# A two-block transformer kernel in split fp32: drain waits, the order of a product's passes, and the places of constants, a recurrent step and latent means

## The chip, the cores and the metric

The kernel runs on one core of a Trainium2 chip. The metric is the device time of one execution, in microseconds; lower is better. A core has TensorE (PE in the profile, with its weight loads as PEld), VectorE (DVE), ScalarE (ACT), GpSimd (POOL) and SyncE (SP). Each works through its own list of instructions in order; they meet at semaphores. SP and ACT also issue DMA transfers, each on a queue of its own.

## What is computed

A sequence of 256 tokens with 1024 channels passes through two blocks, each with two layers. All matrices are fp32.

```python
def first_block(x, ...):                      # per layer
    h = _rmsnorm(x, norm1_g[layer])
    proj = h @ w_in[layer]                    # split into the heads' parts
    o_a = _hgrn2(...)                         # gated recurrence, chunks of 64
    o_b = _nsa(...); o_c = _fox(...)          # two kinds of attention
    x = x + concatenate([o_a, o_b, o_c]) @ w_o[layer]
    h2 = _rmsnorm(x, norm2_g[layer])
    x = x + square(relu(h2 @ w_up[layer])) @ w_down[layer]

def second_block(x, c, ctx, c_ctx, ...):      # per layer; hc is the context stream
    h = h + HALF * gt1 * swiglu(ada_norm(h, g_ffn1[l], sh1, sc1), w1, w3, w2)
    u = ada_norm(h, g_mix[l], sh2, sc2)
    z_conv, z_cq, z_ckv, z_kr, z_four = split_mixing(u @ w_in[l])
    # latent attention: rms_norm(z_cq) @ w_uq, rms_norm(z_ckv) @ w_ukv
    y = merge_branches(u, conv_module(z_conv, ...), attn @ w_o_mla[l],
                       fourier_mix(z_four, ...), w_bgate[l], b_bgate[l], w_out[l])
    h = h + gt2 * y
    h = h + HALF * gt3 * swiglu(ada_norm(h, g_ffn2[l], sh3, sc3), w1, w3, w2)
```

`swiglu` is `(silu(x @ w1) * (x @ w3)) @ w2`; `merge_branches` is `(g0*y_conv + g1*y_mla + g2*y_four) @ w_out` with sigmoid gates. In the second block's first layer the context stream goes through the same steps, so the tiles there are 512 wide (256 tokens of each stream); in its second layer most are 256 wide.

## The kernel before

**Weights.** The weights come as one stream of chunks, mostly 128 x 1024 fp32 (512 KB: eight tiles of 128 x 128), through a ring of four slots. SP issues each load (L2614) when PE has released the slot (`used`). `PLAN` gives each product its place in the stream: `in_t`, `up`, `down`, `ffn1`, `ffn1_out`, `conv_in`, `lat_in`, `mix_out` and so on. A product has `n` groups of 128 output channels, each with one to four chunks.

**Split products.** Where a product is split, a chunk is made into two parts: ACT copies it, rounded, into `w_hi` (`split_high`, L749), and DVE writes the rest, `w_lo`, over the ring slot (`split_low`, L773). The activations are split in the same way (`hn_hi`/`hn_lo`, `hid_hi`/`hid_lo`, `mrg_hi`/`mrg_lo`). `split_product` (L802) makes three matmuls for each of the eight tiles: low weights by high activations (L812), high by high (L815), high by low (L818). Before, all eight of L812 come first and then the pairs. Parts are made some groups ahead (`splits_ahead`, `early`, `shift`).

**Banks.** Groups alternate between two pairs of PSUM banks. `wait_banks` makes PE wait until the group two before has been drained; `wait_all_drained` waits for the last two groups of a product.

**Feed-forward of the second block.** `gated_pair` makes 22 groups of ffn1 or ffn2. ACT applies Silu to one bank, DVE multiplies by the other (L2160, which frees the banks), copies to `hid_hi` (L2163) and subtracts for `hid_lo` (L2166). Then comes the out-projection (`hidden_product`), whose first chunk reads rows 0 to 7.

**Merging.** The last branch, mrg_mla, ends for each of 8 groups with a gate (L2263), an addition (L2269, which frees the banks), the copy to `mrg_hi` (L2273) and the subtraction to `mrg_lo` (L2275). mix_out reads all eight rows in its first group, each behind a wait for its `mrg_lo`.

**in_t with the recurrence.** block1 makes 18 groups of in_t on PE while DVE and ACT run the recurrence in turns tied to group numbers: in group 3 DVE does the forget gate (`hg_start_dve`, L1306 to L1313, which needs ACT's two sigmoids of L1405/L1406), in group 5 the scan, and from group 6 on a step every two groups: two subtractions (`hg_grow_dve`, L1341/L1345), an exponential on ACT (L1414), two products (`hg_decay_dve`, L1361/L1362), sixteen small matmuls on PE (`hg_pe`, L1276), and the taking of the scores (`hg_take_dve`, L1374), for which PE's next step waits. In each group DVE first makes the low part that is due and then the step's work.

**Start.** x, the small constants and the parameters are loaded first. ACT issues the large constants (L1617) and the context (L1618) after the first norm. DVE needs the constants in group 3 of in_t, PE in group 7.

**Latent part.** After conv_in (three groups of two chunks) come ten groups of lat_in, while DVE runs 31 convolution taps (L2523, L2526). ACT copies each group into z (L2417) and squares some. PE then makes two means (L2309, L2312), ACT turns each into a reciprocal root (L2426, L2428), and PE and ACT run the Fourier steps: step u writes bank 4 + u % 2 (L2200, second stage L2208), ACT copies it (L2218), and step u waits for copy u - 2; the second stage waits for all copies of the first. There are 8 first-stage steps in layer 0 and 4 in layer 1. DVE applies the roots (`latent_normed`) at tap 22.

Of the kernel before, what the change touches and what calls it, by code (L numbers as in the profile page):

```python
# [30 lines left out]
T = 256  # L31
# [515 lines left out]
def kernel_program(nc, streams, consts, params, x_cm, ctx_cm, out_cm, blocks=(1, 2)):  # L547
    with ExitStack() as stack:
# [253 lines left out]
        def split_product(pe, lin, g, c, dst, wait_part, x_hi, x_lo, start=True, stop=True, order=None):  # L802

            wait_split(pe, lin, g, c)
            slot = slot_of(lin, g, c)
            order = order or range(lin.tiles[c])
            for k in order:
                if g.at == 0:  # L810
                    wait_part(0, k)
                pe.matmul(dst, w_lo[slot][:, k * P:(k + 1) * P], x_hi(k), start=(start and k == order[0]), stop=False)  # L812
            for k in order:
                high = w_hi[:, slot, k * P:(k + 1) * P]
                pe.matmul(dst, high, x_hi(k), start=False, stop=False)  # L815
                if g.at == 0:
                    wait_part(1, k)
                mm = pe.matmul(dst, high, x_lo(k), start=False, stop=(stop and k == order[-1]))  # L818
            mm.then_inc(used[slot], 1)
# [792 lines left out]
        def block1_act(act, l):  # L1612
            if l == 0:
                first_split(split_high, act, PLAN["in_t", 0])
            norm_act(act, 2 * l, PLAN["in_t", l], PLAN["down", l - 1] if l else None)
            if l == 0:
                act.dma_start(con12[:, 0:CONST_SETS[1][1]], consts[1]).then_inc(s.consts1, 16)  # L1617
                act.dma_start(res[:, :, T:2 * T], ctx_cm).then_inc(s.ctx_in, 16)  # L1618
                act.wait_ge(s.lb, 1)
                act.activation(lb, lb, ACT.Exp).then_inc(s.lb, 1)  # L1620
# [70 lines left out]
            norm_act(act, 2 * l + 1, PLAN["up", l], PLAN["wo", l])  # L1691
            if l == DEPTH - 1 and 2 in blocks:
                act.wait_ge(s.norm_value, KT * 2 * DEPTH)
                act.dma_start(con12[:, 0:CONST_SETS[2][1]], consts[2]).then_inc(s.consts2, 16)
                act.dma_start(par12[:, 0:PARAM_SETS[2][1]], params[2]).then_inc(s.consts2, 16)
                act.dma_start(crow, params[3]).then_inc(s.crow_in, 16)
# [111 lines left out]
        def block1_dve(dve, l):  # L1808
# [6 lines left out]
            for m in range(lin.n):  # L1815
                splits_ahead(split_low, dve, lin, Group(m, m, 0, period(1)))
                if m == SLOT_F and l == 0:
                    dve.wait_ge(s.consts1, 16)
                hg_dve(dve, l, m)
            for m in range(2):  # L1820
                hg_dve(dve, l, IN_SLOTS + m)
# [273 lines left out]
        def ffn_pe(pe, l, which):  # L2095
            n = 2 * DEPTH + 3 * l + which
            w = norm_width(n)
            lin = PLAN["ffn1" if which == 0 else "ffn2", l]
            norm_pe(pe, n)
            gated_pair(pe, lin, n, w)  # L2100
            wait_all_drained(pe, lin)
            lin = PLAN["ffn1_out" if which == 0 else "ffn2_out", l]
            for g in turns(pe, lin):
                wait_banks(pe, lin, g)
                hidden_product(pe, lin, g, FF2 * (2 * l + which // 2), w)
# [85 lines left out]

        def fourier_pe(pe, l):
            wait_all_drained(pe, PLAN["lat_in", l])
            for u, stage, a, tt, gp in fourier_steps(l):
# [17 lines left out]

        def fourier_act(act, l):
            for u, stage, a, tt, gp in fourier_steps(l):
# [77 lines left out]
        def block2_pe(pe, l):  # L2292
# [14 lines left out]
            pe.wait_ge(s.c_sq, l + 1)  # L2307
            for k in range(3):
                mm = pe.matmul(bank[6][:, 0:w], const(2, "ones_ct"), q2[:, 3 + k, 0:w], start=(k == 0), stop=(k == 2))  # L2309
            mm.then_inc(s.c_ms, 1)  # L2310
            for k in range(2):
                mm = pe.matmul(bank[7][:, :], const(2, "ones_kv"), q2[:, 6 + k, :], start=(k == 0), stop=(k == 1))  # L2312
            mm.then_inc(s.c_ms, 1)
# [76 lines left out]
            wait_all_drained(pe, PLAN["mrg_mla", l])  # L2390
            lin = PLAN["mix_out", l]
            for g in turns(pe, lin):
                wait_banks(pe, lin, g)
                split_product(pe, lin, g, 0, bank[2 * parity(lin, g)][:, 0:w],
                              lambda part, k: pe.wait_ge(s.mrg_lo, KT * l + k + 1),
                              lambda k: mrg_hi[:, k, 0:w], lambda k: mrg_lo[:, k, 0:w])
            ffn_pe(pe, l, 2)

        def block2_act(act, l):
# [24 lines left out]
            for i, (b, wi) in enumerate(((6, w), (7, 2 * T))):  # L2424
                act.wait_ge(s.c_ms, 2 * l + i + 1)
                act.activation(tmp3[:, i, 0:wi], bank[b][:, 0:wi], ACT.Ln, bias=eps_col)  # L2426
                act.drain()
                last = act.activation(tmp3[:, i, 0:wi], tmp3[:, i, 0:wi], ACT.Exp, scale=-0.5)  # L2428
            last.then_inc(s.c_rs, 1)
# [71 lines left out]
        def block2_dve(dve, l):  # L2501
# [6 lines left out]
            for g in turns(dve, lin, tail=2):  # L2508
                splits_ahead(split_low, dve, lin, g)
# [6 lines left out]
            if seqs(l) == 1:  # L2516
                first_split(split_low, dve, PLAN["lat_in", l])
# [211 lines left out]
```

## Time and profile before

| | us |
|---|---|
| median of 3 runs | 2947.27 (2946.25 to 2950.39) |
| profiled execution | 2950.16 |
| its span, first to last instruction | 2948.4 |
| mean granted TensorE clock | 0.987 |

| engine | busy us | share of the span |
|---|---|---|
| PE | 2840.2 | 96% |
| DVE | 1644.5 | 56% |
| ACT | 1124.3 | 38% |
| POOL | 48.1 | 2% |

The span is that of the profiled execution; its own time is 1.8 us longer. PE is busy nearly all the time, so the other engines' idle time costs nothing unless PE waits for them. A clock of 1.00 is TensorE's full clock (2.4 GHz), 0.50 is half of it (1.2 GHz).

### The profile page before, as it was taken

The numbers are of one execution on the slowest core, as the hardware profiler recorded it, in microseconds if no ns is written. First come the engines' busy times: TensorE is split into PE (matmuls) and PEld (weight loads), VectorE is DVE, ScalarE is ACT, GpSimd is POOL, SyncE is SP. The second block draws the span as 40 slices with busy tenths as digits, with TensorE's granted clock in tenths as the row PEclk, the third lists the DMA queues.
The fourth block names the chain that finished last, engine by engine and source line by source line (L and its number), as shares of the span: only waits on it lengthen the run. The fifth ranks groups of instructions, "written<-read, shape, count | busy, mean of one in ns | idle before, by whom it ended". The sixth has DMA issues, their size and how long they took to land.

```text
span 2948.4 us, 44779 instructions
## 1 busy us (share of the span) xinstructions
PE 2840.2 (96%) x16592; PEld 2370.8 (80%) x16592; DVE 1644.5 (56%) x2829; ACT 1124.3 (38%) x1715; POOL 48.1 (2%) x36
## 2 busy tenths in 40 slices
PE   7999999999999999999999999999999998999998
PEld 7759998659998888785666778888788887788998
DVE  6547656447666555677334476555533336745665
ACT  4345534345542222324544232222322223584443
POOL 0100001000000000030000000000000000000000
PEclk9999999999999999999999999999999999999999
DMA  5574554655544343321221233433322222234454
GB/s 186 182 247 144 184 182 130 221 210 196 185 157 145 140 150 128 121 91 40 76 68 54 96 112 139 149 133 132 105 94 98 91 96 98 89 112 144 164 183 152
DMA packets 118357, 400.08 MB, mean 136 GB/s; under 512 B 12896, under 2 KB 20960, under 8 KB 117856
## 3 DMA queue, kind: packets, MB, share of 16 engines
q1 hardware_dynamic: 115120, 391.43, 39.1%
q10 hardware_dynamic: 3120, 7.07, 0.7%
q8 instruction: 76, 1.25, 0.2%
q14 instruction: 41, 0.34, 0.0%
HBM read 397.40 MB, written 1.05 MB: 135 GB/s over the span
## 4 chain that ended last, share of the span: by engine, by line
PE 84%; DVE 6%; DMA 3%; ACT 3%; issue 2%; DVEq 1%; POOL 1%; SPq 0%; ACTq 0%; POOLq 0%
PE bank L812 23%; PE bank L815 22%; PE bank L818 22%; PE bank L2234 4%; DMA ring<-weights 3%; PE bank L1534 2%; DVE w_lo L773 1%; PE bank L1979 1%; PE bank L1959 1%; DVE hn_lo L1019 1%; DVE work L2048 1%; PE bank L899 1%; ACT w_hi L749 1%; PE bank L1463 1%; POOL w_lo L773 1%
## 5 line engine op out<-in xcount | busy, mean ns | idle before, releaser
L773 DVE TENSOR_TENSOR w_lo<-ring,w_hi 128x1024 fp32r<-128x1024 f32 (+1 forms) x538 | 650.0, 1209 | 720.8 <-ACT w_hi L749 718.5
L749 ACT ACTIVATE w_hi<-ring 128x1024 fp32r<-128x1024 f32 (+1 forms) x548 | 571.4, 1044 | 1172.5 <-DMA ring<-weights 1172.2
L815 PE MATMUL bank<-hn_hi,w_hi 128*128 128x256 f32 (+1 forms) x2816 | 885.1, 334 | 0.0
L818 PE MATMUL bank<-hn_lo,w_hi 128*128 128x256 f32 (+1 forms) x2816 | 884.6, 334 | 0.0
L815 PEld LDWEIGHTS bank<-hn_hi,w_hi 128*128 128x128 f32 x2816 | 536.9, 191 | 52.2
L818 PEld LDWEIGHTS bank<-hn_lo,w_hi 128*128 128x128 f32 x2816 | 536.8, 191 | 52.2
L812 PE MATMUL bank<-hn_hi,w_lo 128*128 128x256 f32 (+1 forms) x2816 | 559.0, 341 | 15.0 <-DVE w_lo L773 5.6
L812 PEld LDWEIGHTS bank<-hn_hi,w_lo 128*128 128x128 f32 x2816 | 445.5, 191 | 84.7 <-issue 19.8
L815 PE MATMUL bank<-hid_hi,w_hi 128*128 128x512 f32 (+1 forms) x704 | 248.7, 363 | 0.0
L818 PE MATMUL bank<-hid_lo_a,w_hi 128*128 128x512 f32 (+1 forms) x640 | 226.2, 363 | 0.0
L812 PE MATMUL bank<-hid_hi,w_lo 128*128 128x512 f32 (+1 forms) x704 | 156.8, 363 | 4.9 <-DVE work L2160 4.9
L815 PEld LDWEIGHTS bank<-hid_hi,w_hi 128*128 128x128 f32 x704 | 132.9, 189 | 20.6
L812 PEld LDWEIGHTS bank<-hid_hi,w_lo 128*128 128x128 f32 x704 | 121.7, 189 | 26.7 <-issue 5.1
L818 PEld LDWEIGHTS bank<-hid_lo_a,w_hi 128*128 128x128 f32 x640 | 120.8, 189 | 18.7
L815 PE MATMUL bank<-up_hi,w_hi 128*128 128x256 f32 x512 | 125.6, 283 | 0.0
L818 PE MATMUL bank<-up_lo,w_hi 128*128 128x256 f32 x512 | 125.6, 283 | 0.0
L2234 PE MATMUL bank<-hid,ring 128*128 128x512 f32 (+1 forms) x352 | 124.2, 494 | 1.3 <-ACT hid L2023 1.3
L2526 DVE SCALAR_TENSOR_TENSOR hid<-work,par,hid 128x512 f32<-128x512 f32 (+1 forms) x180 | 117.4, 707 | 5.0 <-issue 0.5
L815 PEld LDWEIGHTS bank<-up_hi,w_hi 128*128 128x128 f32 x512 | 98.3, 192 | 0.0
L818 PEld LDWEIGHTS bank<-up_lo,w_hi 128*128 128x128 f32 x512 | 98.3, 192 | 0.0
L2234 PEld LDWEIGHTS bank<-hid,ring 128*128 128x128 f32 x352 | 63.8, 189 | 42.7 <-issue 38.3
L1456 PE MATMUL bank<-hn_hi,w_lo 128*128 128x256 f32 (+1 forms) x160 | 63.5, 405 | 28.4 <-ACT hn_hi L994 16.9
(320 smaller groups left out, 3006.3 us busy)
## 6 DMA issues: line engine op xcount, KB each, us to landing
ring<-weights SPq DMA_DIRECT2D x692, 512.0 KB, 3.3
ring<-weights SPq DMA_DIRECT2D x32, 384.0 KB, 3.0
ring<-weights SPq DMA_DIRECT2D x32, 256.0 KB, 2.6
ring<-weights SPq DMA_DIRECT2D x28, 192.0 KB, 2.3
con<-consts ACTq DMA_DIRECT2D x1, 2063.0 KB, 7.4
con<-consts ACTq DMA_DIRECT2D x1, 1088.0 KB, 5.0
res<-ctx_cm ACTq DMA_DIRECT2D x1, 1024.0 KB, 14.1
con<-params ACTq DMA_DIRECT2D x1, 1024.0 KB, 7.1
```

The source lines that it names most:

```text
L749: act.activation(w_hi[:, slot, 0:w], ring[slot][:, 0:w], ACT.Copy).then_inc(s.w_hi, 1)
L773: eng.tensor_tensor(w_lo[slot][:, 0:w], ring[slot][:, 0:w], w_hi[:, slot, 0:w].bitcast(F32), ALU.subtract).then_inc(s.w_lo, 1)
L812: pe.matmul(dst, w_lo[slot][:, k * P:(k + 1) * P], x_hi(k), start=(start and k == order[0]), stop=False)
L815: pe.matmul(dst, high, x_hi(k), start=False, stop=False)
L818: mm = pe.matmul(dst, high, x_lo(k), start=False, stop=(stop and k == order[-1]))
L899: mm = pe.matmul(ada_bank(h)[rows, :], cs[:, k, COND_AT - 2 * q:COND_W - 2 * q], ring[slot][:, i * 4 * P:(i + 1) * 4 * P], start=(q == 0 a ...
L1019: last = dve.scalar_tensor_tensor(out=hn_lo[:, k, t], in0=sq[:, k, t], scalar=modulation(l)[:, SHIFT[which], k, c:c + 1], in1=hn_hi[:, k, ...
L1456: pe.matmul(dst[c], w_lo[slot[c]][:, k * P:(k + 1) * P], hn_hi[:, k, 0:w], start=(k == 0), stop=False)
L1463: mm = pe.matmul(dst[c], w_hi[:, slot[c], k * P:(k + 1) * P], hn_lo[:, k, 0:w], start=False, stop=(k == KT - 1))
L1534: mm = pe.matmul(bank[2 * parity(lin, g)][:, q], sq[:, k, q], ring[slot_of(lin, g, 0)][:, k * P:(k + 1) * P], start=(k == 0), stop=(k == K ...
L2234: mm = pe.matmul(bank[2 * parity(lin, g)][:, 0:w], ring[slot_of(lin, g, 0)][:, k * P:(k + 1) * P], src[:, k, 0:w], start=(k == 0), stop=(k ...
L2526: last = dve.scalar_tensor_tensor(out=dst, in0=src, scalar=taps[:, m, k:k + 1], in1=dst, op0=ALU.mult, op1=ALU.add)
```

## The change

- `ffn_pe` and `block2_pe` no longer call `wait_all_drained` between ffn1/ffn2 and the out-projection and between mrg_mla and mix_out.
- `split_product` can go row by row (`by_row`): for each tile its low pass and its two high passes. mix_out uses it.
- ACT issues the large constants behind its first high part, ahead of the first norm, and the context after the second norm of the first layer.
- In in_t, DVE does the recurrent step of a group ahead of the low part due in that group.
- The latent means move into the Fourier steps on PE, ahead of step 2; on ACT the roots move ahead of the copy of step 3.
- In the last layer, the first low part of lat_in moves into conv_in's last group, ahead of its gate.

```diff
-        def split_product(pe, lin, g, c, dst, wait_part, x_hi, x_lo, start=True, stop=True, order=None):
+        def split_product(pe, lin, g, c, dst, wait_part, x_hi, x_lo, start=True, stop=True, order=None, by_row=False):
...
-            for k in order:
+            def low_pass(k):
                 if g.at == 0:
                     wait_part(0, k)
                 pe.matmul(dst, w_lo[slot][:, k * P:(k + 1) * P], x_hi(k), start=(start and k == order[0]), stop=False)
-            for k in order:
+
+            def high_passes(k):
                 high = w_hi[:, slot, k * P:(k + 1) * P]
                 pe.matmul(dst, high, x_hi(k), start=False, stop=False)
                 if g.at == 0:
                     wait_part(1, k)
-                mm = pe.matmul(dst, high, x_lo(k), start=False, stop=(stop and k == order[-1]))
-            mm.then_inc(used[slot], 1)
+                return pe.matmul(dst, high, x_lo(k), start=False, stop=(stop and k == order[-1]))
+
+            if by_row and g.at == 0:
+                for k in order:
+                    low_pass(k)
+                    mm = high_passes(k)
+            else:
+                for k in order:
+                    low_pass(k)
+                for k in order:
+                    mm = high_passes(k)
+            mm.then_inc(used[slot_of(lin, g, c)], 1)
...
         def block1_act(act, l):
             if l == 0:
                 first_split(split_high, act, PLAN["in_t", 0])
+                act.dma_start(con12[:, 0:CONST_SETS[1][1]], consts[1]).then_inc(s.consts1, 16)
             norm_act(act, 2 * l, PLAN["in_t", l], PLAN["down", l - 1] if l else None)
             if l == 0:
-                act.dma_start(con12[:, 0:CONST_SETS[1][1]], consts[1]).then_inc(s.consts1, 16)
-                act.dma_start(res[:, :, T:2 * T], ctx_cm).then_inc(s.ctx_in, 16)
...
             norm_act(act, 2 * l + 1, PLAN["up", l], PLAN["wo", l])
+            if l == 0:
+                act.dma_start(res[:, :, T:2 * T], ctx_cm).then_inc(s.ctx_in, 16)
...
             for m in range(lin.n):
-                splits_ahead(split_low, dve, lin, Group(m, m, 0, period(1)))
                 if m == SLOT_F and l == 0:
                     dve.wait_ge(s.consts1, 16)
                 hg_dve(dve, l, m)
+                splits_ahead(split_low, dve, lin, Group(m, m, 0, period(1)))
...
             gated_pair(pe, lin, n, w)
-            wait_all_drained(pe, lin)
...
+        def latent_means(pe, l):
+            w = seqs(l) * T
+            pe.wait_ge(s.c_sq, l + 1)
+            for k in range(3):
+                mm = pe.matmul(bank[6][:, 0:w], const(2, "ones_ct"), q2[:, 3 + k, 0:w], start=(k == 0), stop=(k == 2))
+            mm.then_inc(s.c_ms, 1)
+            for k in range(2):
+                mm = pe.matmul(bank[7][:, :], const(2, "ones_kv"), q2[:, 6 + k, :], start=(k == 0), stop=(k == 1))
+            mm.then_inc(s.c_ms, 1)
         def fourier_pe(pe, l):
             wait_all_drained(pe, PLAN["lat_in", l])
-            for u, stage, a, tt, gp in fourier_steps(l):
+            for n, (u, stage, a, tt, gp) in enumerate(fourier_steps(l)):
+                if n == 2:
+                    latent_means(pe, l)
...
+        def latent_rstd(act, l):
+            w = seqs(l) * T
+            for i, (b, wi) in enumerate(((6, w), (7, 2 * T))):
+                act.wait_ge(s.c_ms, 2 * l + i + 1)
+                act.activation(tmp3[:, i, 0:wi], bank[b][:, 0:wi], ACT.Ln, bias=eps_col)
+                act.drain()
+                last = act.activation(tmp3[:, i, 0:wi], tmp3[:, i, 0:wi], ACT.Exp, scale=-0.5)
+            last.then_inc(s.c_rs, 1)
+
         def fourier_act(act, l):
-            for u, stage, a, tt, gp in fourier_steps(l):
+            for n, (u, stage, a, tt, gp) in enumerate(fourier_steps(l)):
+                if n == 3:
+                    latent_rstd(act, l)
                 act.wait_ge(s.f_mm, u + 1)
...
-            wait_all_drained(pe, PLAN["mrg_mla", l])
             lin = PLAN["mix_out", l]
...
-                              lambda k: mrg_hi[:, k, 0:w], lambda k: mrg_lo[:, k, 0:w])
+                              lambda k: mrg_hi[:, k, 0:w], lambda k: mrg_lo[:, k, 0:w], by_row=True)
...
             for g in turns(dve, lin, tail=2):
-                splits_ahead(split_low, dve, lin, g)
+                splits_ahead(split_low, dve, lin, g, PLAN["lat_in", l] if seqs(l) == 1 else None)
...
-            if seqs(l) == 1:
-                first_split(split_low, dve, PLAN["lat_in", l])
```

The removed lines of the old means (PE) and of the old roots (ACT) are those of the new functions.

## Rows read from the trace of the kernel before

**Rows 1.** The page, busy time of PE, its share and instructions.

```profile
PE 2840.2 (96%) x16592; PEld 2370.8 (80%) x16592; DVE 1644.5 (56%) x2829; ACT 1124.3 (38%) x1715; POOL 48.1 (2%) x36
```

**Rows 2.** Waits of PE: line <- who ended it: us in total, times, longest.

```profile
PE bank L1276 <- DVE hid L1374: 7.1, 4, 3.1
...
PE bank L812 <- ACT hid L1626: 5.3, 4, 4.1
...
PE bank L812 <- DVE work L2160: 4.9, 4, 1.3
PE bank L812 <- DVE work L2269: 4.8, 2, 2.8
...
PE bank L812 <- issue: 2.4, 1, 2.4
```

**Rows 3.** Stretches: length, busy PE, PEld, DVE, ACT, POOL, granted clock, DMA share, GB/s.

```profile
1668.70:1672.10 3.40, 3.34 (x8) 2.70 (x9) 2.40 (x3) 1.06 (x1) 0.00 (x0) 0.50 0.01 5
1672.20:1675.60 3.40, 3.40 (x16) 2.79 (x15) 0.00 (x0) 0.00 (x0) 0.00 (x0) 1.00 0.00 0
2719.40:2722.80 3.40, 3.40 (x31) 3.40 (x29) 2.37 (x5) 1.06 (x1) 0.00 (x0) 1.00 0.11 36
```

**Rows 4.** The page's DMA issues; ACT's timeline and a stretch of the start.

```profile
ring<-weights SPq DMA_DIRECT2D x692, 512.0 KB, 3.3
...
con<-consts ACTq DMA_DIRECT2D x1, 2063.0 KB, 7.4
...
12.66 1.06 ACT L749 ACTIVATE w_hi<-ring 128x1024 fp32r<-128x1024 f32 x1 [0.22 <-DMA ring<-weights]
...
18.19 0.33 ACTq L1617 DMA_DIRECT2D con<-consts  x1
...
29.30 1.06 ACT L749 ACTIVATE w_hi<-ring 128x1024 fp32r<-128x1024 f32 x1 [5.18 <-DMA ring<-weights]
...
18.90:20.00 1.10, 1.10 (x7) 1.10 (x6) 1.10 (x4) 0.00 (x0) 0.00 (x0) 0.50 1.02 210
```

**Rows 5.** DVE's timeline in in_t, second layer (start, us); last, a steady stretch.

```profile
461.45 0.41 DVE L1306 TENSOR_SCALAR work<-work,small 128x256 f32<-128x256 f32 x1
...
463.63 0.43 DVE L1313 TENSOR_SCALAR work<-work 128x512 f32<-128x512 f32 x1
...
475.83 1.22 DVE L773 TENSOR_TENSOR w_lo<-ring,w_hi 128x1024 fp32r<-128x1024 f32 x1
...
477.82 1.33 DVE L1374 COPY_PREDICATED hid<-con,bank 128x512 f32<-128x512 uint32 x2
479.82 1.23 DVE L773 TENSOR_TENSOR w_lo<-ring,w_hi 128x1024 fp32r<-128x1024 f32 x1 [0.66 <-ACT w_hi L749]
...
63.36:77.44 14.08, 14.08 (x131) 13.57 (x129) 10.15 (x16) 6.08 (x10) 0.00 (x0) 1.00 0.47 150
```

**Rows 6.** DVE's timeline before mix_out, first and second layer.

```profile
1668.77 0.69 DVE L2275 TENSOR_TENSOR mrg_lo<-work,mrg_hi 128x512 fp32r<-128x512 f32 x1
...
1670.25 1.23 DVE L773 TENSOR_TENSOR w_lo<-ring,w_hi 128x1024 fp32r<-128x1024 f32 x1
...
2719.55 1.23 DVE L773 TENSOR_TENSOR w_lo<-ring,w_hi 128x1024 fp32r<-128x1024 f32 x1
```

**Rows 7.** DVE's timeline at the end of conv_in, second layer.

```profile
2477.45 1.23 DVE L773 TENSOR_TENSOR w_lo<-ring,w_hi 128x1024 fp32r<-128x1024 f32 x1 [0.45 <-ACT w_hi L749]
2482.39 0.42 DVE L2512 TENSOR_TENSOR work<-bank,work 128x256 f32<-128x256 f32 x1 [3.71 <-ACT work L2409]
```

**Rows 8.** Timeline of PE and ACT behind lat_in, first layer.

```profile
1335.58 2.74 PE L2309 MATMUL bank<-hid,con 128*128 128x512 f32 x6
1335.77 0.60 ACT L2417 ACTIVATE hid<-bank 128x512 f32<-128x512 f32 x1 [4.84 <-PE bank L818]
...
1338.35 0.69 ACT L2426 ACTIVATE work<-bank,small 128x512 f32<-128x512 f32 x1 [0.68 <-PE bank L2309]
...
1340.82 0.63 ACT L2428 ACTIVATE work<-work 128x512 f32<-128x512 f32 x1
...
1341.99 5.63 PE L2200 MATMUL bank<-con,hid 128*128 128x256 f32 x24 [0.24 <-ACT work L2218]
...
1348.40 1.10 PE L2208 MATMUL bank<-con,work 128*128 128x256 f32 x4 [0.78 <-ACT work L2218]
```

More of the change, by code:

```diff
@@ L2305, in block2_pe @@
                 input_product(pe, lin, g, 0, bank[2 * parity(lin, g)][:, 0:wg], n + 1, wg)
[L2307 to L2313, printed above, removed]
             fourier_pe(pe, l)
@@ L2423, in block2_act @@
             act.preload_act_table_set(LOG_EXP)
[L2424 to L2429, printed above, removed]
             fourier_act(act, l)
```

## The prediction

> **What bounds the kernel now.** I read the page's busy shares first: TensorE (PE) is busy 2840.2 of 2948.4 us, 96% [rows 1]. Nothing in the change removes a matmul, so it can only work on the other 108 us, and on matmuls that run at half clock. The next view is the waits of PE: the reader is to look at who ended each wait, and how often. Five of its lines name places that the diff touches [rows 2]. The third view is the granted clock in stretches behind such waits [rows 3]: after the wait of 2.8 us ahead of the mixed output the clock is 0.50 for 3.4 us, with 8 matmuls in that stretch against 16 in the next one as long; after 2.0 us (second layer) it stays 1.00. So a removed wait of 2.4 us or more (the shortest of those here behind which the clock fell) also gives back half of 3.4, 1.7 us. That price returns wherever a new wait of that size arises. Last come the timelines of ScalarE (ACT) and VectorE (DVE) around each place: the question is what would be late next.
>
> **The change part by part.** Positive is time saved; "first" and "second" are the layers l=0 and l=1 of a block.
>
> *Last gating (ffn_pe).* PE no longer waits until both last groups of ffn1/ffn2 are drained. wait_banks still asks for group 20, drained one group earlier, and the first chunk's rows 0 to 7 are long written. The wait on the gating multiply L2160 is 4.9 us over 4 times, at most 1.3 [rows 2]. Late next is the low part of the second chunk: about 1 us early in the three wide stages, 0.1 us late in the narrow one. Saved 4.8, bounds 4 and 5.
>
> *Mixed output (by_row, no drain wait).* 2.8 us in the first layer, 2.0 in the second [rows 2]. First layer: after the change PE starts when group 7's products end (1666.0). Row 7's low part comes at 1669.46 [rows 6]; ahead of it lie 7 rows of 3 matmuls, 21 of 0.23 us, or 4.8 us, so it is in time. Without by_row only 7 matmuls lie ahead, 1.6 us, and the wait would return at row 7. The next weight group's low part ends at 1671.48 [rows 6], PE wants it at 1671.4: a new wait of about 0.2. With the half clock saved: 2.8 + 1.7 - 0.2 = 4.3. Second layer: matmuls are 0.12 us, the first group is done at 2719.3, but the next group's low part only ends at 2720.78 [rows 6], behind the same DVE work as before. PE started that group at 2721.3 and now can at 2720.9: saved 0.4. Together 4.7, bounds 3 (no half clock saved) and 6.5 (both waits whole).
>
> *Constants (norm_act) and context.* The two transfers (2063 and 1024 KB) are issued at 18.2 and 18.6 us, just ahead of weight chunk 4. ACT gets this chunk only at 29.30, after 5.18 us of idling for the DMA [rows 4]; a weight load takes 3.3 us as a rule [rows 4]. PE then waits 4.1 us (the longest of L812 for ACT L1626, [rows 2]), and half clock follows: 5.8 us. Now the constants go out at about 11.2, behind ACT's first high part, and flow until about 18 to 19 (7.4 us to landing, [rows 4]), while PE waits on the norm anyway; the DMA is idle by 14. DVE (group 3) and PE (group 7) need them after 28 us. The context goes out at about 256, in a stretch without loads up to 261; at 1 MB and some 390 GB/s it needs 2.6 us of data time: nothing, bound 1.0. Its one reader comes hundreds of us later.
> What it costs: ACT issues for 0.33 us where it would idle 0.21 for chunk 1, and chunk 2 has just landed at 12.63 [rows 4]. Issued at 18.2, the first constants move within 0.9 us (210 GB/s from 18.9, [rows 4]), so now from about 12.1, with the end of chunk 2 still to come. Chunk 2 carries the start (its high part, then the norm). I take -0.5, bounds 0 and -1.5.
> The Trainium skill, "DMA: Bandwidth & Descriptors", section "Queues, rings and completion order", has a rule against this edit: each DMA engine goes round between the queues it has work for, a whole packet at a time, so a queue with large packets takes its turns among the weight packets. The trace agrees as far as chunk 4 goes, which moved little until the constants were through [rows 4].
>
> *Recurrent step ahead of low parts (block1_dve).* In group 8 of in_t, DVE makes the low part of weights (1.22), then the step's two subtractions, then takes the scores (1.33), for which PE stands still 3.1 us [rows 2, 5]. With the step first, the take ends at least 1.2 us earlier, and the same swap at groups 6 and 7 brings exponentials, copies and high parts forward too: the take is done about 1.5 us before PE asks. Saved per layer 3.0 and 1.7 for the half clock, and two small ones: 0.7 in the first layer, 0.4 + 0.3 in the second. Late next is group 5's low part: it now stands behind the forget-gate step of group 3, 2.6 us [rows 5], which starts when ACT has both sigmoids (459.06). Low part 5 is then ready at 463.0 instead of 461.54, and PE wanted it at 462.36: a new wait of 0.7. Second layer: 5.4 - 0.7 = 4.7.
> First layer with the constants gone: 5.8 + 3.0 + 1.7 + 0.7 = 11.2. But chunk 4 no longer hides the sigmoids. PE waits 0.7 for the bank that ACT drains behind them (as in the second layer), about 1.4 behind the forget-gate step, and 0.5 for the start: 8.6, bounds 6 and 11.
> In the steady part a pair of groups with its scores takes PE 7.04 us (14.08 us of busy PE for two, [rows 5]); DVE's two low parts, step and take need 5.3 there. A low part now ends 3.3 us after the scores at which DVE may wait, and PE wants it 7 us after them. No cost.
>
> *First latent low part (conv_in, second layer).* The low part of lat_in's first group was made after the last gate; PE waited 2.4 us for it ("issue", [rows 2]) and half clock followed. ACT has its high part by 2478.4 and DVE idles from 2478.7 to 2482.4 [rows 7], so the work is free there. The taps start 1.1 us earlier than before while PE starts 2.3 earlier; low part 1 is ready at 2485.1, PE wants it at 2487.4. Saved 2.4 + 1.7 = 4.0.
>
> *Latent means inside the Fourier steps.* This edit has no wait to remove: PE goes from L2309/L2312 straight into the Fourier matmuls, with waits of 0.24 and 0.78 in all [rows 8]. What it does is worse. (a) fourier_pe begins with the wait for the last lat_in copy, which ends 0.63 us behind the last product (1336.37 against 1335.74) [rows 8]; the means covered it. Cost 0.7. (b) ACT takes the copy of step 2 ahead of latent_rstd, and step 2 stands behind the means (4.3 us) on PE. So ACT idles during the means, copies step 2, and then needs 2.8 us for the two logarithms and exponentials (1338.35 to 1341.45 less 0.3 of waiting, [rows 8]). PE meanwhile has steps 3 and 4 only (0.94 each), since step 5 needs the bank of step 3. 0.6 (copy) + 2.8 + 0.6 (copy 3) - 1.9 gives a new wait of 2.1 to 2.2. First layer: -0.7 - 2.2 + 0.1 = -2.8. Second layer: there are only four such steps, and the second stage needs all four copies: 0.6 + 2.4 + 0.6 - 0.95, a wait of 2.7, in place of 0.78, and 0.4 for (a): -2.3. That wait is past 2.4, so half clock: -1.7. I leave the first layer's 2.2 below it. Sum -6.8, bounds -8.5 (half clock twice) and -3 (ACT's copy not behind PE's means as I read it).
>
> **Sum.** 4.8 + 4.7 + 8.6 + 4.7 + 4.0 - 6.8 = 20.0 us. The profiled execution took 2950.2 (span 2948.4 and 1.8 around it), which would become 2930.2. The median of before is 2947.3, 2.9 below the profiled one, so I predict 2927.5.
>
> **Rivals.**
> 1. *The Fourier edit costs nothing.* Then 26.8 is saved: 2920.5. For it: ACT is idle half the time there. Against: the order on ACT's one queue. Chance 0.12.
> 2. *The recurrent chain binds again in in_t*, at another step, because exponentials wait behind high parts on ACT (in rows 5 DVE idles 0.66 for one). One wait of 3 with its half clock stays in each layer: 9.4 less, 2937. Chance 0.18.
> 3. *The constants hold up the start.* Their data hold chunk 2 until they are half through: 3 to 4 us instead of 0.5, half of 2063 KB taking 2.7 at 390 GB/s: 2930.5. For it: what happened to chunk 4. Against: nearly all of chunk 2 has moved by 12.1. Chance 0.08. (This is what the rule of the Trainium skill named above would make of the start.)
> 4. *The drain wait isn't what PE waited for*: wait_banks or the second chunk holds it as long, and the two removals give only the clock: 2934. Against: L2160 and L2269 end the waits in rows 2. Chance 0.04.
> 5. *Slower: low parts starve PE in in_t.* DVE now waits for PE's scores ahead of each low part. There are 8 steps in each of 2 layers; the low part has 3.7 us to spare. If a step's turn on ACT and DVE took 5.7 us longer than I read, each would cost 2: 32 - 20 = 12 slower, 2959. It decides from 1.25 us per step. Against: DVE is busy only 10.2 of 14.1 us there. Chance 0.03.
>
> **How the numbers follow.** The forecast has 0.55; its own range is 2922 to 2933, from half clocks (1.7 each) that fall or don't at four places and the bounds of the start. To hold 8 in 10 I add rival 1 in part and rivals 2 and 3: 2919 to 2938. What a measurement here can tell from no change is about 0.2%, 5.9 us. Faster by more: all of the forecast and rivals 1 to 4 but for tails, 0.94. Within it: 0.03, slower: 0.03.
>
> **What would show it.** In the changed profile: L2160 and L2269 gone from PE's waits, L812 on mrg_hi without a wait and a clock of 1.00 behind it; chunk 4's high part near 26 us and no wait of 4 us at 29; no wait of L1276 over 1 us; a new wait of L812 on w_lo of about 1 us at group 5; the wait of 2.4 at lat_in gone; and L2200 with a new wait of about 2.2, L2208 with 2.7, both ended by ACT L2218. I am wrong if the Fourier steps show no new wait, or if in_t keeps one of 3 us.

## The result and the profile after

The changed kernel took 2924.24 us (median of 4 runs, 2921.88 to 2929.6) where the kernel before took 2948.1 on the same chip (4 runs): ratio 0.9921, 95% interval 0.9904 to 0.9938, 23 us less. A second measure on another chip gave 2925.57 (5 runs) against 2945.89 (9 runs): 0.9928 (0.9915 to 0.9942). The forecast was 2927.5, range 2919 to 2938. The profiled execution of after took 2923.91 us, span 2922.1, against 2950.16 and 2948.4: 26.3 less, where 20.0 was forecast.

The page after, answering to [rows 1]:

```profile
PE 2832.6 (97%) x16592; PEld 2367.1 (81%) x16592; DVE 1641.7 (56%) x2829; ACT 1125.5 (39%) x1715; POOL 47.0 (2%) x36
```

PE's idle time fell from 108.2 to 89.5 us, and its busy time by 7.6 with the same 16592 matmuls. Most of the 7.6 is half clock: 68.2 us of PE's busy time lay in stretches at half clock before, 56.2 after, and half of the difference is 6.0.

Waits of PE in the changed kernel (line <- who ended it: total, times, longest), answering to [rows 2]:

```profile
PE bank L812 <- DVE w_lo L773: 8.5, 9, 2.1
...
PE bank L2230 <- ACT work L2251: 3.3, 2, 2.5
...
PE bank L2222 <- ACT work L2251: 1.9, 1, 1.9
...
PE bank L812 <- ACT hid L1636: 1.5, 2, 0.8
...
PE bank L2222 <- ACT hid L2442: 0.8, 1, 0.8
```

The lines have moved: the scores' matmul L1276 is L1287 now, the Fourier steps L2200 and L2208 are L2222 and L2230. All five lines of [rows 2] are gone but the one for ACT's bank copy (L1626, now L1636), which fell from 5.3 us with a longest of 4.1 to 1.5 with a longest of 0.8. New are the waits for ACT at the Fourier steps: 6.0 us in three lines, where before had 2.1 there (1.6 and 0.5). The wait for low parts (w_lo) grew from 5.6 to 8.5: 0.61 and 0.46 of it come in in_t and 1.39 at the second mixed output, as the prediction foresaw; the longest, 2.07 at 678 us, lies outside the change.

Stretches of the changed kernel at the places of [rows 3] (length, busy PE, PEld, DVE, ACT, POOL, granted clock, DMA share, GB/s): the beginning of the mixed output in the first layer, then behind the new wait of 2.5 us in the second layer:

```profile
1648.40:1651.80 3.40, 3.40 (x17) 2.82 (x16) 0.00 (x0) 0.59 (x2) 0.00 (x0) 1.00 0.06 22
...
2508.50:2511.90 3.40, 3.40 (x16) 3.01 (x17) 3.27 (x7) 0.39 (x1) 0.00 (x0) 1.00 0.02 5
```

The first row has 17 matmuls at clock 1.00, against 8 at 0.50. The second row is the surprise: half clock was forecast here, and it didn't come.

ACT's timeline at the start of the changed kernel (start, us), and its DMA issues, answering to [rows 4]:

```profile
9.24 1.06 ACT L749 ACTIVATE w_hi<-ring 128x1024 fp32r<-128x1024 f32 x1 [4.85 <-DMA ring<-weights]
9.24 0.33 ACTq L1626 DMA_DIRECT2D con<-consts  x1
...
13.35 1.06 ACT L749 ACTIVATE w_hi<-ring 128x1024 fp32r<-128x1024 f32 x1 [1.74 <-DMA ring<-weights]
...
27.75 1.06 ACT L749 ACTIVATE w_hi<-ring 128x1024 fp32r<-128x1024 f32 x1 [1.86 <-DMA ring<-weights]
...
con<-consts ACTq DMA_DIRECT2D x1, 2063.0 KB, 10.3
```

Timelines of the changed kernel at the Fourier steps, first layer (PE, ACT, PE) and second layer (PE), answering to [rows 8]:

```profile
1329.23 1.06 ACT L2251 ACTIVATE work<-bank 128x512 f32<-128x512 f32 x2
...
1329.87 2.95 PE L2222 MATMUL bank<-con,hid 128*128 128x256 f32 x12 [1.90 <-ACT work L2251]
1333.59 2.61 PE L2230 MATMUL bank<-con,work 128*128 128x256 f32 x11 [0.78 <-ACT work L2251]
...
2508.49 1.75 PE L2230 MATMUL bank<-con,work 128*128 128x256 f32 x7 [2.52 <-ACT work L2251]
```

Where the 26.3 us came from is read by how far each stage's first matmul of after stands ahead of the same matmul of before:

| from, to (us in before) | what lies in it | gained | forecast |
|---|---|---|---|
| 0 to 16.0 | start up to the first pair | -0.7 | -0.5 |
| 16.0 to 134.6 | in_t, first layer | 8.3 | 9.1 |
| 134.6 to 442.0 | modulation, norms, matmuls without the change | 2.0 | 0 |
| 442.0 to 559.7 | in_t, second layer | 6.2 | 4.7 |
| 559.7 to 873.4 | without the change | 0.9 | 0 |
| four ends of ffn | last gating | 0.75, 1.6, 1.6, 1.2 | 4.8 in all |
| 1317.7 to 1348.4 | Fourier, first layer | -2.7 | -2.8 |
| 1348.4 to 1716.8 | mixed output, first layer | 4.2 | 4.3 |
| 2453.3 to 2514.4 | conv_in, second layer | 4.1 | 4.0 |
| 2514.4 to 2532.8 | Fourier, second layer | -2.0 | -4.0 |
| 2532.8 to 2743.9 | mixed output, second layer | 0.7 | 0.4 |

### The profile page after: what moved, and what is told of

Same layout as the page of the kernel before. It is cut to its first block, busy times and chain, and to the rows that moved or that the text cites. A ratio compares the mean times of both kernels' runs of the same rounds, so it can differ in the third digit from the quotient of the medians.

```text
span 2922.1 us, 44773 instructions
## 1 busy us (share of the span) xinstructions
PE 2832.6 (97%) x16592; PEld 2367.1 (81%) x16592; DVE 1641.7 (56%) x2829; ACT 1125.5 (39%) x1715; POOL 47.0 (2%) x36
## 3 DMA queue, kind: packets, MB, share of 16 engines
HBM read 397.40 MB, written 1.05 MB: 136 GB/s over the span
## 4 chain that ended last, share of the span: by engine, by line
PE 87%; DVE 4%; DMA 3%; ACT 2%; issue 2%; POOL 1%; DVEq 1%; SPq 0%; ACTq 0%; POOLq 0%
PE bank L812 23%; PE bank L819 23%; PE bank L816 23%; PE bank L2267 4%; DMA ring<-weights 3%; PE bank L1545 2%; PE bank L1991 1%; PE bank L1971 1%; DVE w_lo L773 1%; DVE work L2060 1%; DVE hn_lo L1030 1%; PE bank L2350 1%; PE bank L910 1%; PE bank L2230 1%; PE bank L1467 1%
## 5 line engine op out<-in xcount | busy, mean ns | idle before, releaser
L812 PE MATMUL bank<-hn_hi,w_lo 128*128 128x256 f32 (+1 forms) x2816 | 556.5, 340 | 10.2 <-DVE w_lo L773 7.1
L812 PEld LDWEIGHTS bank<-hn_hi,w_lo 128*128 128x128 f32 x2816 | 443.9, 190 | 79.3 <-issue 17.8
L812 PE MATMUL bank<-hid_hi,w_lo 128*128 128x512 f32 (+1 forms) x704 | 156.4, 362 | 0.0
L812 PEld LDWEIGHTS bank<-hid_hi,w_lo 128*128 128x128 f32 x704 | 121.9, 189 | 20.6
## 6 DMA issues: line engine op xcount, KB each, us to landing
con<-consts ACTq DMA_DIRECT2D x1, 2063.0 KB, 10.3
```

## Experiments

Each kernel is the changed one with the edit shown, compared with the kernel before on its own chip. To compare them with each other I use the ratio, as the chips differ (before: 2945.9 to 2948.1).

| run | median (range, runs), us | ratio, 95% interval |
|---|---|---|
| changed | 2924.24 (2921.88 to 2929.6, 4) | 0.9921, 0.9904 to 0.9938 |
| h1 changed again | 2925.57 (2922.16 to 2929.7, 5) | 0.9928, 0.9915 to 0.9942 |
| f1 means back | 2918.26 (2916.69 to 2919.5, 4) | 0.9902, 0.9886 to 0.9917 |
| g1 means back again | 2917.83 (2917.41 to 2921.12, 4) | 0.9909, 0.9892 to 0.9925 |
| f2 roots first | 2920.42 (2918.37 to 2925.88, 4) | 0.9912, 0.9896 to 0.9927 |
| f3 order back | 2932.61 (2929.46 to 2934.51, 5) | 0.9948, 0.9934 to 0.9961 |
| f4 constants back | 2928.09 (2925.03 to 2933.06, 5) | 0.9937, 0.9924 to 0.9951 |
| f5 no rows | 2925.79 (2923.18 to 2927.48, 6) | 0.9928, 0.9915 to 0.9942 |
| f6 drain waits back | 2937.42 (2928.55 to 2942.8, 10) | 0.9967, 0.9956 to 0.9979 |
| f7 conv back | 2926.68 (2922.72 to 2929.84, 6) | 0.9932, 0.9918 to 0.9947 |
| f8 combined | 2921.13 (2917.97 to 2922.0, 5) | 0.9911, 0.9896 to 0.9926 |
| g2 gate last | 2919.38 (2914.67 to 2927.43, 4) | 0.9906, 0.9890 to 0.9923 |
| g3 constants after | 2918.52 (2916.65 to 2922.24, 4) | 0.9910, 0.9893 to 0.9926 |

**f1, the means ahead of the Fourier steps again.**

```diff
-                if n == 2:
-                    latent_means(pe, l)
-                if n == 3:
-                    latent_rstd(act, l)
+            latent_means(pe, l)
             fourier_pe(pe, l)
+            latent_rstd(act, l)
             fourier_act(act, l)
```

> The changed kernel with the latent means and roots back ahead of the Fourier steps. Theory (the means inside the Fourier steps cost time: the wait for lat_in's last copy is uncovered, and ACT copies step 2 before it makes the roots): PE goes from the products into the means without a wait, the waits of 1.9 (L2222) and 2.5 us (L2230) shrink to about 0.2 and 0.8, and from the end of lat_in to the first second-stage matmul it is 2.6 us shorter in the first layer, 2.0 in the second: 4.6 us faster than the changed kernel, about 2919.5. Rival (the means' place costs nothing, what PE loses there comes back at the next wait): within 1 us of the changed kernel, 2924.

PE's timeline of this kernel in the first layer (start, us):

```profile
1320.16 5.63 PE L2220 MATMUL bank<-con,hid 128*128 128x256 f32 x24 [0.23 <-ACT work L2247]
1326.57 3.69 PE L2228 MATMUL bank<-con,work 128*128 128x256 f32 x16 [0.78 <-ACT work L2247]
```

The steps are as in [rows 8] again, 0.2 and 0.8 us of waiting. By the traces of this kernel and the changed one, the two Fourier stages are 2.7 and 2.0 us shorter, as expected. The medians show 6.0; some of that lies elsewhere, as no half clock came behind the first norm in this profiled execution. The edit inside the Fourier steps is a loss. g1 is the same kernel, measured again beside g2 and g3:

> The changed kernel with the latent means and roots ahead of the Fourier steps again, measured a second time beside the next two kernels, so that the three share a chip. If the result of the first measure was not luck: 2918 (2915.5 to 2920.5). If it was luck (a profiled execution there had no half clock behind the first norm): 2920 or above, as the combined version.

It came to 2917.83. The two ratios of f1 and g1 stand 0.0012 to 0.0026 below the two of the changed kernel, 3.5 to 7.7 us, with intervals that overlap a little. No other version of the case is clearly faster.

**f2, the means stay inside, ACT takes the roots one copy earlier.** This asks whether ACT's order is the cause, as the prediction has it, or the place of the means on PE.

```diff
-                if n == 3:
+                if n == 2:
                     latent_rstd(act, l)
```

> The changed kernel with one line different: ACT makes the roots ahead of the copy of step 2 instead of step 3. If the new waits come from ACT's order (step 2's copy stands behind the means and ahead of the roots), then ACT makes the roots during the means, the waits of 1.9 and 2.5 us fall to under 1, and only the uncovered copy wait (0.8 and 0.5) stays: 3 to 4 us faster than the changed kernel, about 2920.5. Rival (the waits come from the means' place on PE alone, whatever ACT does first): both waits stay within 0.5 us of 1.9 and 2.5.

ACT's and PE's timelines of this kernel, first layer:

```profile
1322.44 0.69 ACT L2239 ACTIVATE work<-bank,small 128x512 f32<-128x512 f32 x1 [1.98 <-PE bank L2207]
...
1326.08 3.81 PE L2222 MATMUL bank<-con,hid 128*128 128x256 f32 x16 [0.24 <-ACT work L2251]
1330.67 3.69 PE L2230 MATMUL bank<-con,work 128*128 128x256 f32 x16 [0.78 <-ACT work L2251]
```

ACT now starts the roots when the first mean is there, not behind a copy whose product stands behind the means. The waits of 1.90 and 2.5 are gone. What stays is the wait for the last copy of lat_in, 0.78 in the first layer and 0.52 in the second. The order on ACT's queue was the cause of the two long waits.

**f3, low part ahead of the recurrent step again.**

```diff
+                splits_ahead(split_low, dve, lin, Group(m, m, 0, period(1)))
                 hg_dve(dve, l, m)
-                splits_ahead(split_low, dve, lin, Group(m, m, 0, period(1)))
```

> The changed kernel with the low part ahead of the recurrent step again in in_t; constants stay early. Theory (DVE's order is what PE waits for at group 8): L1287 waits of about 3 us return in both layers, each with half clock for 3.4 us, and the small waits at group 5 (0.6 and 0.5 on w_lo) go: about 9 us slower than the changed kernel, 2933. Rival (in the first layer the wait at group 8 came from the late chunk 4, and the early constants alone remove it): only the second layer's wait returns, 4.5 us slower, 2929.

Waits of PE in this kernel:

```profile
PE bank L1287 <- DVE hid L1385: 7.1, 4, 3.1
```

The same 7.1, 4, 3.1 as in [rows 2], although the constants come early, with a clock of 0.51 and 0.50 for 3.4 us behind each wait of 3.07. That the early constants alone would free the recurrent chain is thereby refuted. The edit is worth 7.0 to 8.4 us by the medians; in the traces the two in_t stages are 4.8 and 5.2 us longer than in the changed kernel.

**f4, constants and context late again.**

```diff
-                act.dma_start(con12[:, 0:CONST_SETS[1][1]], consts[1]).then_inc(s.consts1, 16)
...
+                act.dma_start(con12[:, 0:CONST_SETS[1][1]], consts[1]).then_inc(s.consts1, 16)
+                act.dma_start(res[:, :, T:2 * T], ctx_cm).then_inc(s.ctx_in, 16)
```

> The changed kernel with the constants and the context issued after the first norm again. Theory: chunk 4's high part waits 5 us for the DMA, PE waits 4.1 us for it and runs at half clock behind it, while the start is 0.7 us earlier (chunk 2 lands 0.7 sooner): 4 to 5 us slower than the changed kernel, 2928.5. Rival (the recurrent chain then has more slack and takes part of it back, since PE comes later to group 8): 2 to 3 us slower, 2926.5.

Waits of PE in this kernel, then ACT's timeline:

```profile
PE bank L812 <- ACT hid L1637: 4.4, 2, 3.8
...
30.25 1.06 ACT L749 ACTIVATE w_hi<-ring 128x1024 fp32r<-128x1024 f32 x1 [4.84 <-DMA ring<-weights]
```

Chunk 4 is late again behind the constants: its load takes 6.3 us from issue (23.96) to landing, 3.3 in the changed kernel, and its high part comes at 30.25 instead of 27.75. PE waits 3.8 us, with half clock behind it. The medians show 2.5 and 3.9 us, but their intervals overlap with those of the changed kernel; in the traces the stage of in_t, first layer, is 3.4 us longer. That lies between theory and rival.

**f5, the drain waits gone but the old order of the passes in the mixed output.**

```diff
-                              lambda k: mrg_hi[:, k, 0:w], lambda k: mrg_lo[:, k, 0:w], by_row=True)
+                              lambda k: mrg_hi[:, k, 0:w], lambda k: mrg_lo[:, k, 0:w])
```

> The changed kernel with mix_out's first product in the old order of passes; the drain waits stay away. Theory (by_row is what makes the removed wait pay): PE does 7 low passes (1.6 us) and then waits 1.9 us for row 7's low part in the first layer, short of what brings half clock, and 1.5 us in the second, where the wait of 1.4 for the next weights then shrinks by as much: 2 us slower than the changed kernel, 2926.5; with half clock behind the first wait 2928. Rival (removing the drain wait is enough): no new wait, 2924.

Waits of PE in this kernel:

```profile
PE bank L812 <- DVE mrg_lo L2308: 3.5, 2, 2.0
```

The wait comes back where the prediction put it, at the low part of row 7: 1.97 us in the first layer (none in the changed kernel) and 1.57 in the second (in place of one of 1.39 for w_lo). The medians differ by 1.6 at most, ratio 0.9928 against 0.9921 and 0.9928: by row is worth about 2 in the trace and can't be told by the times.

**f6, f5 with the five drain waits back.**

```diff
             gated_pair(pe, lin, n, w)
+            wait_all_drained(pe, lin)
...
                 branch_pe(pe, l, 2, g)
+            wait_all_drained(pe, PLAN["mrg_mla", l])
```

> The changed kernel with the drain waits back ahead of the four out-projections and of mix_out, and mix_out's passes in the old order. Theory: PE waits 1.3 us three times and 1.0 once for the last gating (4.8 in all), 2.8 us with half clock ahead of the first mix_out and 2.0 ahead of the second: 9.4 us slower than the changed kernel, 2933.5. Rival (what was saved at these places came back later): under 5 us slower.

Waits of PE, and the stretch behind the one of 2.8:

```profile
PE bank L812 <- DVE work L2172: 4.9, 4, 1.3
PE bank L812 <- DVE work L2303: 4.8, 2, 2.8
...
1661.70:1665.00 3.30, 3.30 (x9) 2.56 (x8) 2.12 (x3) 1.06 (x1) 0.00 (x0) 0.50 0.00 0
```

Both rows are those of [rows 2] to the tenth. The drain waits cost 11.6 us against f5 on the same chip, more than the 7.0 expected. In the profiled pair the difference is 16.8, of which 6.0 has piled up by 855 us, before any of the edits acts (later weights, longer half clock in this execution); the rest, 10.8, lies in the stages with a drain wait. It reads 2.4, 1.5, 1.5 and 2.1 at the ends of the four ffn stages and 2.4 and 1.7 at the two mixed outputs, 11.6, less 0.9 for a shorter half clock behind the norm ahead of conv_in, second layer. Of the 7.5 at the ffn stages 4.9 are the waits themselves; most of the rest is half clock that lasted longer in this execution. The forecast's terms for these edits were 4.8 and 4.7. The ten runs of f6 spread from 2928.55 to 2942.8, and the profiled one is the slowest, so 11.6 is a rough figure; that the waits are back is certain.

**f7, the first latent low part behind the last gate again.**

```diff
-                splits_ahead(split_low, dve, lin, g, PLAN["lat_in", l] if seqs(l) == 1 else None)
+                splits_ahead(split_low, dve, lin, g)
...
+            if seqs(l) == 1:
+                first_split(split_low, dve, PLAN["lat_in", l])
```

> The changed kernel with the last layer's first low part of lat_in behind the last gate of conv_in again. Theory: PE waits 2.4 us ahead of lat_in's first group and half clock follows: 4.1 us slower than the changed kernel, 2928.3. Rival (the taps of the convolution, which start 1.1 us earlier with the change, take part of it back): 2 us slower or less.

Waits of PE in this kernel, then stretches behind the wait of 2.4 and behind the one of 2.5 at the Fourier steps:

```profile
PE bank L812 <- issue: 2.4, 1, 2.4
...
2458.90:2462.20 3.30, 3.30 (x10) 2.55 (x9) 3.13 (x7) 0.00 (x0) 0.00 (x0) 0.50 0.02 5
...
2510.10:2513.40 3.30, 3.30 (x9) 2.56 (x9) 3.13 (x8) 0.38 (x1) 0.00 (x0) 0.50 0.02 5
```

The stage from the norm's wait to L812's wait of 1.65 takes 61.2 us here, 57.0 in both executions of the changed kernel: 4.2 us, the forecast's 4.0. The medians show 1.1 and 2.4, within their spread.

**f8, the best repairs together**: means back, in group 3 of in_t alone the low part first again, and the constants issued behind the first norm's root.

```diff
+            latent_means(pe, l)
             fourier_pe(pe, l)
...
+                if m != SLOT_F:
+                    hg_dve(dve, l, m)
                 splits_ahead(split_low, dve, lin, Group(m, m, 0, period(1)))
+                if m == SLOT_F:
+                    hg_dve(dve, l, m)
...
+            if n == 0:
+                act.dma_start(con12[:, 0:CONST_SETS[1][1]], consts[1]).then_inc(s.consts1, 16)
```

> The changed kernel with three repairs: the latent means and roots ahead of the Fourier steps again (2918.3 measured for this alone), the low part ahead of the forget gate in group 3 only, and the constants issued behind the first norm's root, where ACT idles, not behind the first high part. Theory: chunk 2 lands 0.7 us sooner and the wait on w_lo at group 5 goes (0.5 and 0.6), so 1.8 us less than the first repair: 2916.5. Rival (with the gate 1.2 us later the take of the scores is late at group 8 again, or the constants now run into chunk 4): a wait of L1287 or of L812 for ACT of 1 us or more comes back, 2918 or over.

The sum of repairs failed: 2921.13, not 2916.5. The ratio, 0.9911, can't be told from those of f1 and g1 (0.9902, 0.9909). In its profiled execution the waits of PE for weights were 7.9 us with a longest of 2.2 where f1's were 6.0 with a longest of 0.9:

```profile
PE bank L910 <- DMA ring<-weights: 7.9, 11, 2.2
...
PE bank L812 <- ACT hid L1637: 2.3, 4, 0.8
```

But no wait of L1287 or for chunk 4 is there. So I measured the two repairs one by one, each with the means back, on one chip with g1.

> Means ahead of the Fourier steps, and in group 3 of in_t alone the low part of weights is made ahead of the forget-gate step (the other groups keep the step first). Theory: the waits of 0.6 and 0.46 at the groups behind it shrink, the wait of the low product at group 5 goes, and no wait of L1287 comes; the gain is at most 1 and lost in the spread, so 2918 as the kernel beside it, within 1.5. Rival (this repair is what made the combined version slower): 2921, with a wait of 1 us or more of PE for ACT in in_t.

> Means ahead of the Fourier steps, and the first constants are issued behind the first norm's root rather than behind ACT's first high part. Theory: the first pair starts up to 0.5 earlier and chunk 4 is in time still; 2918 as the kernel beside it, within 1.5. Rival (this repair is what made the combined version slower): the constants now flow into chunks 3 and 4, a wait of 1 us or more comes at about 29, and the time is 2920.5 or above.

They took 2919.38 and 2918.52 beside 2917.83: neither brings or costs anything that the times can show, and by the ratios f8 isn't slower than g1 either. The wait of 0.61 at group 5 goes in g2, but one of 0.75 comes a group later (at 37.2 us). What does differ between single executions is when weights land in the modulation stage, from 125 to 240 us, where DMA is busy 0.60 to 0.62 of the time: the profiled execution of f8 had waits of 1.88, 1.11 and 2.20 us for them, those of f1 and g1 none over 0.9.

**h1, the changed kernel again.**

> The changed kernel itself, measured a second time, as the anchor for all the undone parts. If putting the means back is worth what the traces say (about 4.6 of waits), this stands at 2923 to 2926, ratio near 0.992, and a profile shows the waits of 0.78, 1.90 and 2.5 at the Fourier products again; whether half clock follows the last of these a second time is open: theory of a fixed limit says never (2.53 brought none twice), the rival that it is chance says in some executions. If the first measure was unlucky: 2921 or below, and the repair is worth less than 3.

As expected: 2925.57, and the waits of 0.78, 1.90 and 2.52 stand at the Fourier steps again, the last again without half clock.

## Why the prediction was right, step by step

*Last gating (forecast 4.8).* Right: 0.75, 1.6, 1.6 and 1.2 us, 5.1 in all, and the waits on the gating multiply are gone. The first of the four is masked: the norm ahead of it was followed by 5.8 us of half clock in after and 3.4 in before.

*Mixed output (4.7).* Right in both layers: 4.2 and 0.7 for 4.3 and 0.4. PE didn't wait in the first layer, and the clock stayed at 1.00. In the second layer "late next is the next group's low part" holds: 1.39 us for w_lo where 2.02 was.

*Constants, context and order, first layer (8.6).* Measured 7.6 with the start. The forecast had the high part of chunk 4 near 26; it came at 27.75 here and at 25.62 in h1. The load itself isn't held up any more: 3.3 us from issue (24.44) to landing, 6.6 in before (22.68 to 29.28). It was issued late because PE, after a later start and a longer half clock, released the slot late. The wait of 0.78 that PE has left is the one for the bank, forecast at 0.7. After that it waits 0.61 at group 5, where 1.4 was forecast. Half clock behind the start's wait lasted 5.8 us beyond it instead of 3.4, half of which is 1.2: without this it would be 8.8.

*The start (-0.5).* The size can't be seen, and the working came out by luck. It had the constants issued at 11.2, behind ACT's first high part, and moving 0.9 us later, from 12.1. The queue issued them at 9.24, when that part started, and yet their first packet started only at 12.40: 3.2 us after the issue, where before had 0.95 (18.19 to 19.14). Two errors of about 2 us cancelled. Why the first packet waited wasn't tested. In the ten executions with the early issue (at 9.1 to 10.7) it starts at 12.1 to 12.8, with 148 to 368 of the 1024 KB of chunks 2 and 3 still to land, so most of chunk 2 had moved, as the prediction held against rival 3. The bytes did collide: DMA share 1.05 to 1.16 from 11.5 to 15 us, and the constants landed in 10.3 us where they had taken 7.4. Still, over these ten executions the first pair starts at 16.33 us in the mean (15.6 to 16.7), over the four with a later issue (before, f4, f8, g3) at 16.24 (16.0 to 16.5). Rival 3, 3 to 4 us, is refuted. The rule cited for it, of the Trainium skill, "DMA: Bandwidth & Descriptors", section "Queues, rings and completion order", fits what f4 shows of chunk 4 (30.25 against 27.75), but its price at the start is nil here: chunk 2's high part follows chunk 1's by 1.8 us in the mean of either group (1.3 to 2.8 with the early issue, 1.3 to 2.1 with the later one).

*Order, second layer (4.7).* 6.2, of which 1.1 is a shorter half clock behind the norm (3.4 us beyond the wait for 5.6); 5.1 remains. The new wait at group 5 is 0.46, forecast 0.7. f3 confirms the edit on its own: 8.4 and 7.0 us by the medians for two layers, 10.0 in the traces of the two stages, where the expectation's sum was some 9.

*conv_in (4.0).* 4.1, and 4.2 by f7's trace.

*Means inside the Fourier steps (-6.8).* The mechanism is right at each step: wait for the last copy 0.78 (forecast 0.7), 1.90 (2.2) and 2.5 (2.7), ended by ACT. The failed term is "that wait is past 2.4, so half clock: -1.7". Measured 4.6 (2.66 and 1.99) instead of 6.8. I had taken a length from the waits of before and made a limit of it. The trace of before already spoke against that, outside the rows that the change touches: inside and behind a wait of 2.02 us in the modulation stage the clock is 0.50, while behind the equally long one at the second mixed output it is 1.00 [rows 3]. PE's timeline and the stretch, of the kernel before:

```profile
563.96 2.08 PE L1574 MATMUL bank<-hid,con 128*128 128x512 f32 x2 [2.02 <-DVE work L1397]
...
562.80:566.20 3.40, 2.24 (x3) 1.18 (x4) 1.19 (x3) 0.63 (x1) 0.00 (x0) 0.50 0.92 355
```

In the seven profiled executions with this order of ACT and PE (changed, h1, f3 to f7) the wait of 2.5 us brought half clock once (f7), and the wait of 1.9 us, which I had left below the limit, brought it four times (f3 to f6). f5 shows the latter; the rows are its stretch inside the wait and the one behind it:

```profile
1325.70:1327.40 1.70, 0.00 (x0) 0.00 (x0) 1.62 (x3) 1.63 (x4) 0.00 (x0) 1.00 0.00 0
1328.80:1332.10 3.30, 3.04 (x8) 1.87 (x6) 3.30 (x6) 1.28 (x3) 0.00 (x0) 0.50 0.00 0
```

So the price of half clock is an average over executions, here an estimate of (1 + 4) x 1.7 / 7 = 1.2 for the two waits together, and not 1.7 for every wait past a limit. The profiled execution of after paid none of it.

*The sum.* Terms as measured: 5.1 + 4.9 + 7.6 + 6.2 + 4.1 - 4.6 = 23.3. Against the forecast's 20.0 the largest differences are the means (+2.2), the second layer's order (+1.5) and the first layer (-1.0). The other 3.0 of the 26.3 lie in stages that the change doesn't touch: 2.0 + 0.9 of weights that landed earlier and shorter half clock, and 0.1 of rounding. By the medians the gain is 23.9 (2948.1 to 2924.24) and 20.3 (h1): the forecast of 20.0 was right within the spread. How near it came is in part luck, as half clocks fell otherwise than told and errors of either sign met. (The last step of the sum is off by 0.2: 2930.2 less 2.9 is 2927.3.)

*Rivals.* 1 (the Fourier edit is free) is refuted by f1 and f2. 2 (the recurrent chain binds again): L1287 has no wait in PE's list after. 5 (low parts starve PE): the only waits for low parts in in_t are the 0.61 and 0.46 at group 5. 3 is refuted as told. 4 (PE waited for something else than the drain) is refuted by f5 and f6.

## What to carry to other kernels

When work is moved into a pipeline of another kind, follow the order on the queue of each engine, not the busy share: ACT was idle over half the time, and one copy that stood ahead of the roots made waits of 1.9 and 2.5 us on PE, for a move that had no wait to remove. Removing a wait is worth its length only up to what comes next; here "late next" (the next group's low part, the forget-gate step) was readable in the timeline of before to within 0.8 us. An edit of 2 us is not to be judged by the medians of four to ten runs that spread by 3 to 14 us: the trace of the stage decides, and a difference between two whole spans must first be cleared of stages that neither edit touches.

## What the runs showed of the hardware

- Half clock does not follow from a wait's length. The same wait, with the same matmuls ahead of it, brought it in some executions and not in others: 1.9 us in four of seven, 2.5 us in one of seven, and the norm's wait of 2.5 us at 663 us (682 in before) in ten of the fourteen profiled executions. In the other four, the changed kernel and h1 among them, PE was sooner at a low part some 15 us on, waited 2.0 to 2.1 us for it (0.8 in before), and half clock came there. When it comes it lasts 3.4 or 6.8 us in the records, part of it at times still inside the wait; behind that norm's wait 0, 3.4 or 5.6 to 6.0 us were at half clock. What tells these apart I did not find, and no run was made for it. The Trainium skill, "TensorE: Matmul & The Clock Gate", section "Part 1: The HAM clock gate", says that the number of slow matmuls varies from run to run of one kernel, as the monitor's phase at the start does; these traces agree that it varies, and can't show that phase.
- A DMA that stands behind a compute instruction on ACT's queue is issued when that instruction starts, not when it ends: 9.24 us for both in the changed kernel, and within 0.02 us of each other in all ten executions with that order.
- With weight loads in flight, the first packet of the constants on ACT's queue started 1.6 to 3.2 us after their issue (ten executions; 9.24 to 12.40 in the changed kernel), without them 0.95 to 0.97 (four executions; 18.19 to 19.14 in before). The cause wasn't tested.
- In the modulation stages, where DMA is busy 0.6 of the time, PE waited up to 2.2 us for one weight load in one execution (f8) and at most 0.9 in others (f1, g1). That this and the half clocks make up the spread of the runs is my reading; no run separates them.
